# Hybrid decoder step: paged value loads in another token order, and four edits to the order of the attention work

## Chip, cores and metric

One Trainium2 chip, one NeuronCore. The metric is the device time of one execution of the whole program in microseconds (us), lower is better.

## The reference

Two layers; each is a half-step SwiGLU feed-forward (FFN), a mixing stage and a second half-step FFN. There are two groups of rows: a prompt (1 sequence of 256 tokens) and a sample group (8 sequences of 8 new tokens, each with 1024 cached tokens). Cut to the mixing stage:

```python
z = rmsnorm(x, g_mix) @ w_in                   # 1024 -> 2944 columns: u | qa ka va | qr kr vr gr
y_pool, pool_new = pool_mixer(u, ...)          # 4 groups x 64
past_k = cache_k[l][page_table].reshape(8, 1024, 6, 64)    # 8 pages of 128 tokens per sequence
past_v = cache_v[l][page_table].reshape(8, 1024, 6, 64)
y_att = moba_seq(q, concat(past_k, ka), concat(past_v, va), pos)
    # blocks of 256 keys, each query takes its 3 best past blocks (by q . mean key) and its own,
    # s = q.k / 8 - slope_h * distance, softmax, p @ v
o_r, ret_new = retention(qr, kr / 8, vr, s0)   # chunkwise recurrent, per-head norm, silu gate
x = x + concat(y_pool, y_att, y_ret) @ w_out
```

All of it is float32. Softmax and p @ v add over the keys of a sequence, so the order in which the 128 tokens of a page stand is free as long as scores, distance penalty and values use the same one.

## The kernel before

**The work.** 1024x256-column chunks of weights are loaded by SP's queue (1 MB each, `w_raw`), split by ACT (`w_hi`, L702) and DVE (`w_lo`, L1024; four chunks of the mixing stage by POOL, L643) into two fp32r parts, and multiplied on PE in three passes (L1477 to L1479 in the FFNs, L1597 to L1599 as `mix(c)` for the chunks 0 to 11 of the mixing projection, L1929 to L1931 as the output projection). The moving side is 320 rows: 256 of the prompt, 64 of the sample group.

**The mixing stage** is an order written out by hand for each engine: between the chunks of `mix` stand the parts of the attentions whose inputs are ready. For the sample group's attention the 8 sequences go in 4 pairs p = 0 to 3. Per pair:
- SP and POOL load 16 pages of K, 192 KB each (L410; a page's 128 tokens go to 32 partitions as `"(t r) h d -> t r (h d)"`, four neighbouring tokens to a partition), DVE turns them (`turn_k`, L1143, two halves per sequence), and PE multiplies 48 times (`sample_scores(p)`: L1745 the cached keys, L1757 the new ones) into PSUM banks 2 and 3. There the four tokens of a partition come out as `r t`: token t*4+r is column 32*r+t of its page.
- DVE adds the penalty (`soft_in(p)`, L1215 to L1222; L1216 is the large addition, which at the same time writes the columns back from `r t` into `t r`, the tokens' own order), then finds blocks, maxima and biases (`soft_bias`), and ACT takes the exponentials (`exps(p, parts)`, L861, nine parts).
- PE transposes the probabilities (L1766, L1772) and multiplies them with the value pages (`smp_out(p)`, L1791). The 8 pages of sequence u are loaded by SP (u = 0, 3, 4, 6; L472 and L473) or POOL (u = 1, 2, 5, 7; L656 and L657), 128 tokens to 128 partitions, 1536 bytes each. `smp_out(p)` waits on the arrival counts of all pages of u = 2p and 2p + 1.

The prompt's attention has 6 heads: scores (`scores(i)`, two heads), the maxima of them on DVE (`smax(h)`, L1174 to L1178, which counts `s_max`), exponentials on ACT, transposes on PE (`transpose_p`, L1667). The sample scores of pairs 1, 2 and 3 wait on `s_max`, and `scores(0)` on `sm_in`, which `soft_in` counts.

**SP's queue** in the mixing stage: K pages of pair 1, weight chunks 3 to 6, ..., K pages of pair 3 after `sample_scores(2)` has counted `sc_done`, V pages of u = 0, V pages of u = 3 and 4 after the scores of pair 3, two chunks of `w_out` after `smp_out(0)`, V pages of u = 6, stores of the retention states (L489, L494), two more chunks of `w_out`, then the weights of the second FFN. DMAs of a queue are issued in that order and are not waited for.

**ACT's queue** carries five small loads at the start (L750 to L754): gains, as 16, 16, 16, 8 and 4 rows of 512 bytes.

The V loads differ from the K loads in the pattern only:

```python
A["cache_k"][L, page[j]].rearrange("(t r) h d -> t r (h d)", r=4)   # L411, K: 32 x 4 x 384
A["cache_v"][L, page[j]].rearrange("t h d -> t (h d)")              # L473, L657, V: 128 x 384
```

Of the kernel before, what the change touches and what calls it, by code (L numbers as in the profile page):

```python
# [16 lines left out]
ALU = mybir.AluOpType  # L17
# [13 lines left out]
H = 6  # L31
# [82 lines left out]
def build(nc, A, C, O):  # L114
    ctx = ExitStack()

    def sb(name, shape, dt=F32):
        return ctx.enter_context(nc.sbuf_tensor(name, shape, dt))
# [4 lines left out]
    with ctx:  # L123
# [12 lines left out]
        cst = {n: sb(n, list(C[n].shape)) for n in C}  # L136
# [66 lines left out]
        sp = [sp_a, sp_b, sp_d, sp_a]  # L203
# [52 lines left out]
        s_done, s_max, s_exp, p_norm = sem("s_done"), sem("s_max"), sem("s_exp"), sem("p_norm")  # L256
# [13 lines left out]
        v_landed = {n: sem("v_landed_" + n) for n in "QCWXABDE"}  # L270
        V_HOME = "XQWABCED"
# [85 lines left out]
        def _(sp_e):  # L357
# [43 lines left out]
            for L in range(DEPTH):  # L401
# [65 lines left out]
                def load_v(u, n=PAGES, halves=range(2)):  # L467

                    for half in halves:
                        page = page_numbers(mybir.EngineType.SP, u * PAGES + 4 * half, min(4, n - 4 * half))  # L470
                        for j in range(min(4, n - 4 * half)):
                            sp_e.dma_start(v_page(u, 4 * half + j, slice(0, HDIM)),  # L472
                                           A["cache_v"][L, page[j]].rearrange("t h d -> t (h d)")).then_inc(v_landed[V_HOME[u]], 16)  # L473

                for half in range(2):
                    wait_apart(sp_e, split_done, L * C_ALL + (C_MIX + half + 13))
# [44 lines left out]
        def _(pool):  # L521
# [47 lines left out]
            for L in range(DEPTH):  # L569
# [39 lines left out]
                for n, w in enumerate(WINDOWS):  # L609
# [8 lines left out]
                    o, t = HD * (n % 2), n // 2  # L618
# [34 lines left out]
                def load_v(u, half, first=0, n=4):  # L653
                    page = page_numbers(mybir.EngineType.Pool, u * PAGES + 4 * half + first, n)
                    for j in range(n):
                        pool.dma_start(v_page(u, 4 * half + first + j, slice(0, HDIM)),  # L656
                                       A["cache_v"][L, page[j]].rearrange("t h d -> t (h d)")).then_inc(v_landed[V_HOME[u]], 16)  # L657

                for c in range(8, 12):
                    mix_lo(c)  # L660
# [36 lines left out]
        def _(act):  # L697
# [88 lines left out]
            for L in range(DEPTH):  # L786
# [34 lines left out]
                def vr_tokens(t):  # L821
                    n = P if t < 2 else SMP
                    act.wait_ge(vr_tr, 3 * L + (t + 1))
                    act.activation(vr_tok[0:n, t, :], ps[0:n, VR_BANK[t], 0:HDIM], ACT.Copy).then_inc(vr_out, 1)
# [29 lines left out]
                def exps(p, parts=range(9)):  # L854
                    if 0 in parts:
                        act.wait_ge(sm_bias, L * 4 + p + 1)
                    for k in parts:
                        n, part = divmod(k, 3)
                        a, b = (256 * n + P * part, 256 * n + P * part + P) if part < 2 else (768 + 32 * n, 800 + 32 * n)
                        at_b = 32 * part + n  # L860
                        ins = act.activation(sp[p][:, a:b], sp[p][:, a:b], ACT.Exp, bias=bias_s[:, at_b:at_b + 1],  # L861
                                             accum_out=blk[:, at_b:at_b + 1])
                    if 8 in parts:
                        ins.then_inc(sm_exp, 1)
# [77 lines left out]
                probs_out(5)  # L942
                act.wait_ge(evac_done, L * G_ALL + (GROUPS0 + G_MIX + 12))
                act.activation(z[:, ZG:ZG + 3, :], z[:, ZG:ZG + 3, :], ACT.Silu).then_inc(g_silu, 1)
                exps(3, range(4))
                out_evac(0)
                act.wait_ge(stored_va, 16 * (L + 1))
                att_evac(2)
                exps(3, range(4, 9))
                for t in range(3):  # L950
                    vr_tokens(t)
                for t in range(2):
                    act.wait_ge(pool_mm, 2 * L + (t + 1))
                    act.activation(h_hi[:, t, :], ps[:, 6 + t, 0:TOK], ACT.Copy, scale=gains[:, bass.ds(L * 2 + (NORMS * KT + t), 1)]).then_inc(pool_hi, 1)
# [65 lines left out]
        def _(dve):  # L1020
# [113 lines left out]
            for L in range(DEPTH):  # L1134
# [4 lines left out]
                def turn_k(p, bb, half):  # L1139

                    dve.wait_ge((k_landed[k_home(p, bb)] if p else k_first[bb])[half], k_count(L, p))
                    keys = kbuf[k_home(p, bb)][:, 4 * half:4 * half + 4, :].rearrange("p j c -> p (j c)")
                    dve.transpose(keys, keys).then_inc(kt_ok, 1)  # L1143
# [12 lines left out]
                def evac_first(c):  # L1156
                    dve.wait_ge(tile_done, L * 11 + (c + 1))
                    to_z(2 * c, 2 if c == 1 else 0).then_inc(mix_half, 1)
# [6 lines left out]
                def mix_lo(c):  # L1165
                    lo_split(half0 + (C_MIX + c) // 2, c % 2)
# [44 lines left out]
                def soft_in(p):  # L1211

                    dve.wait_ge(own_done, L * 4 + p + 1)
                    raw = ps[:, 2:4, :].rearrange("p b n -> p (b n)")
                    dve.tensor_reduce(past_blocks(0), raw[:, 0:768].rearrange("p (n k x) -> p n k x", n=3, k=2), AX, ALU.add)  # L1215
                    dve.tensor_tensor(sp[p][:, 0:768].rearrange("p (k t r) -> p k r t", k=6, r=4),  # L1216
                                      raw[:, 0:768].rearrange("p (k r t) -> p k r t", k=6, r=4),
                                      cst["alibi_s"][:].rearrange("p (k r t) -> p k r t", k=6, r=4), ALU.add)
                    dve.tensor_tensor(sp[p][:, 768:864], raw[:, 768:864], cst["alibi_own"][:, p, :], ALU.add).then_inc(sm_in, 1)
                    dve.drain()  # L1220
                    dve.tensor_reduce(past_blocks(2), sp[p][:, 0:768].rearrange("p (n k x) -> p n k x", n=3, k=2), AX, ALU.max)
                    dve.tensor_reduce(blk[:, 128:131], sp[p][:, 768:864].rearrange("p (n x) -> p n x", n=3), AX, ALU.max)  # L1222
                    dve.drain()
# [80 lines left out]
                soft_bias(0)  # L1304
                evac_last(4)
                turn_k(1, 1, 0)
                mix_lo(6)
                turn_k(1, 1, 1)
                smax(0)
                dve.drain()  # L1310
                smax(1)
# [32 lines left out]
                                                cst["q_decay"][o:o + HD, f, :].rearrange("p (b t) -> p b t", b=NB), ALU.mult)  # L1344
                ins.then_inc(q_dec_ok, 1)
                dve.wait_ge(stored_u, 32 * (L + 1))
                soft_in(2)
                evac_first(9)
                soft_bias(2)
                evac_last(9)  # L1350
                turn_k(3, 0, 0)
# [112 lines left out]
        def _(pe):  # L1464
# [102 lines left out]
            for L in range(DEPTH):  # L1567
# [7 lines left out]
                def mix(c, tiles=None):  # L1575

                    if not tiles or 0 in tiles:
                        chunk_split(half0 + (C_MIX + c) // 2, c % 2)
                    tiles = tiles or range(2 if c < 11 else 1)
                    steps = [(a, k) for a in tiles for k in range(KT)]  # L1580
                    if c == 0:
                        steps.sort(key=lambda step: step[1] // 2)
                    for a, k in steps:
                        if c in FETCH and a == tiles[-1] and a == 1 and k == 3:
                            pe.addr_align(BLOCK, FETCH[c], 0)
                        if k == 0:
                            if c < 2:
                                banks_free(L, G_MIX)
                            elif a == 0:
                                pe.wait_ge(mix_half, L * 11 + c)  # L1590
                            else:
                                pe.wait_ge(evac_done, L * G_ALL + (GROUPS0 + G_MIX + c))
                        if c == 0 and a == 0 and k % 2 == 0:
                            pe.wait_ge(gx_ready, (norm + 1) * 4 + (k // 2 + 1))
                        w = slice((k * (2 if c < 11 else 1) + a) * P, (k * (2 if c < 11 else 1) + a + 1) * P)
                        out = ps[:, a + (2 if c == 1 else 0), 0:TOK]
                        pe.matmul(out, w_hi[:, c % 2, w], h_hi[:, k, :], start=(k == 0), stop=False)  # L1597
                        pe.matmul(out, w_hi[:, c % 2, w], h_lo[:, k, :], start=False, stop=False)  # L1598
                        ins = pe.matmul(out, w_lo[:, c % 2, w], h_hi[:, k, :], start=False, stop=(k == KT - 1))  # L1599
                        if k == KT - 1:  # L1600
                            ins.then_inc(tile_done if a == 0 and c < 11 else chunk_used, 1)
# [230 lines left out]
                mixed(4)  # L1832
                u_tokens()
                tokens(ZKA, 0, 7).then_inc(ka_tr, 1)
                pe.wait_ge(sm_in, L * 4 + 1)
                scores(0)
                mix(5)
                pe.wait_ge(ka_out, 3 * L + 1)
                tokens(ZKA, 1, 7).then_inc(ka_tr, 1)
                pe.wait_ge(s_max, H * L + 2)  # L1840
                sample_scores(1)
                mix(6)
                mixed(6)
# [9 lines left out]
                pe.wait_ge(va_out, 3 * L + 2)  # L1853
                att_out(0)
                tokens(ZVA, 2, 6).then_inc(va_tr, 1)
                pe.wait_ge(s_max, H * L + 4)
                sample_scores(2)
                mix(9)
                pe.wait_ge(oa_out, 3 * L + 1)
                tokens(ZKA, 2, 7).then_inc(ka_tr, 1)  # L1860
                transpose_p(2)
# [9 lines left out]
                att_out(1)  # L1871
                transpose_p(4)
                transpose_p(5)
                pe.wait_ge(s_max, H * L + 6)
                sample_scores(3)
                mix(11)

# [150 lines left out]
```

## Time and profile before

| | |
|---|---|
| runs, us | 1321.41, 1322.69, 1322.31 (median 1322.31) |
| profiled execution, us | 1318.97 (span 1317.1, mean granted PE clock 0.995) |
| busy share of the span | PE 98%, DVE 60%, ACT 50%, POOL 18% |
| first FFN and mixing stage, layer 0 | 0 to 254.5 us, 254.5 to 404 us |
| second FFN of layer 0 and first of layer 1 | 404 to 899.7 us |
| mixing stage and second FFN, layer 1 | 899.7 to 1051 us, 1051 to 1317 us |

The profile is of one execution. Its span is the time from the first to the last instruction; 1.9 us of the execution lie outside it. A row of a timeline gives start, duration, engine, line, operation, output and inputs, and in brackets how long the engine was idle before it and what released it. "SPq" and "POOLq" rows are the issue of a DMA, not its transfer. In a view of windows, "DMA" is the mean busy share of the core's 16 DMA engines, GB/s what they moved; records that straddle a window's edge can bring it over 1. PEclk is the TensorE clock that was granted, as a share of full speed (2.4 GHz).

### The profile page before, as it was taken

Reading aid. Unit: us, or ns where it says so; the run is one execution under the profiler, and the core shown is the slowest. Engines: PE = TensorE matmul, PEld = TensorE weight load, DVE = VectorE, ACT = ScalarE, POOL = GpSimd, SP = SyncE. Lnnn points to the kernel's source line nnn. Section 1 sums busy time; section 2 is a strip of 40 time slices with the busy share of each in tenths; the row PEclk is TensorE's granted clock in tenths of the full one; section 3 lists DMA queues with packets and bytes.
Section 4 is the critical chain, followed back from the end, with each engine's and each line's share of the span. In section 5 each row is a group of like instructions: output and inputs, shape, how many; then the busy total and the mean of one; then the engine's idle time right before and its main releaser. Section 6 shows DMA issues by size and latency. Waiting matters only on the chain.

```text
span 1317.1 us, 25155 instructions
## 1 busy us (share of the span) xinstructions
PE 1291.6 (98%) x9881; PEld 1243.8 (94%) x9881; DVE 787.9 (60%) x885; ACT 660.3 (50%) x838; POOL 237.3 (18%) x389
## 2 busy tenths in 40 slices
PE   9999999998999999999999999999899999999998
PEld 7999999997869999999999999999797799999998
DVE  6555555677876655554465555566877675555433
ACT  6555543345464655543365554333446455555433
POOL 1021000358541000000110000013855220000010
PEclk9999999999999999999999999999899999999999
DMA  6676544668994444444456554447599834444441
GB/s 202 203 199 193 167 140 153 187 171 209 284 343 156 136 159 149 138 152 144 151 166 187 165 183 145 150 150 202 142 253 311 292 128 160 144 143 159 144 148 68
DMA packets 201671, 232.97 MB, mean 177 GB/s; under 512 B 15006, under 2 KB 192936, under 8 KB 201604
## 3 DMA queue, kind: packets, MB, share of 16 engines
q1 hardware_dynamic: 194172, 209.10, 51.1%
q0 software_dynamic: 7312, 22.95, 5.9%
q8 instruction: 42, 0.69, 0.2%
q14 instruction: 25, 0.20, 0.1%
q10 hardware_dynamic: 120, 0.03, 0.0%
HBM read 226.83 MB, written 5.32 MB: 176 GB/s over the span
## 4 chain that ended last, share of the span: by engine, by line
PE 85%; DVE 6%; DMA 2%; ACT 2%; DVEq 2%; issue 1%; SPq 1%; ACTq 0%
PE ps L1477 24%; PE ps L1478 24%; PE ps L1479 24%; DMA kbuf<-in_cache_k 2%; PE ps L1597 2%; PE ps L1599 2%; PE ps L1598 2%; DVE w_lo L1024 1%; PE ps L1745 1%; SPq L410 1%; DVE kbuf L1143 1%; PE ps L1929 1%; ACT w_hi L702 1%; DVEq L1220 1%; PE ps L1931 1%
## 5 line engine op out<-in xcount | busy, mean ns | idle before, releaser
L702 ACT ACTIVATE w_hi<-w_raw 128x2048 fp32r<-128x2048 f32 x167 | 319.9, 1915 | 514.3 <-PE ps L1479 415.2
L1024 DVE TENSOR_TENSOR w_lo<-w_raw,w_hi 128x2048 fp32r<-128x2048 f32 x159 | 365.9, 2301 | 196.5 <-ACT w_hi L702 192.0
L1477 PE MATMUL ps<-h_hi,w_hi 128*128 128x320 f32 x768 | 237.9, 310 | 0.8 <-DVE h_lo L1112 0.7
L1479 PE MATMUL ps<-h_hi,w_lo 128*128 128x320 f32 x768 | 237.3, 309 | 0.0
L1478 PE MATMUL ps<-h_lo,w_hi 128*128 128x320 f32 x768 | 237.3, 309 | 0.0
L1477 PE MATMUL ps<-g_hi,w_hi 128*128 128x320 f32 x704 | 217.9, 309 | 0.0
L1479 PE MATMUL ps<-g_hi,w_lo 128*128 128x320 f32 x704 | 217.4, 309 | 0.0
L1478 PE MATMUL ps<-g_lo,w_hi 128*128 128x320 f32 x704 | 217.4, 309 | 0.0
L1478 PE MATMUL ps<-act_lo,w_hi 128*128 128x320 f32 x704 | 217.2, 309 | 0.0
L1477 PE MATMUL ps<-act_hi,w_hi 128*128 128x320 f32 x704 | 217.2, 309 | 0.0
L1479 PE MATMUL ps<-act_hi,w_lo 128*128 128x320 f32 x704 | 217.2, 309 | 0.0
L1477 PEld LDWEIGHTS ps<-h_hi,w_hi 128*128 128x128 f32 x768 | 144.2, 188 | 2.1 <-issue 1.5
L1478 PEld LDWEIGHTS ps<-h_lo,w_hi 128*128 128x128 f32 x768 | 144.2, 188 | 0.1
L1479 PEld LDWEIGHTS ps<-h_hi,w_lo 128*128 128x128 f32 x768 | 144.2, 188 | 0.0
L1477 PEld LDWEIGHTS ps<-g_hi,w_hi 128*128 128x128 f32 x704 | 132.4, 188 | 0.2
L1478 PEld LDWEIGHTS ps<-g_lo,w_hi 128*128 128x128 f32 x704 | 132.3, 188 | 0.2
L1479 PEld LDWEIGHTS ps<-g_hi,w_lo 128*128 128x128 f32 x704 | 132.4, 188 | 0.0
L1478 PEld LDWEIGHTS ps<-act_lo,w_hi 128*128 128x128 f32 x704 | 132.0, 187 | 0.0
L1477 PEld LDWEIGHTS ps<-act_hi,w_hi 128*128 128x128 f32 x704 | 132.0, 187 | 0.0
L1479 PEld LDWEIGHTS ps<-act_hi,w_lo 128*128 128x128 f32 x704 | 132.0, 187 | 0.0
L1597 PE MATMUL ps<-h_hi,w_hi 128*128 128x320 f32 x368 | 116.4, 316 | 0.2 <-DVE z L1154 0.2
L1599 PE MATMUL ps<-h_hi,w_lo 128*128 128x320 f32 x368 | 113.7, 309 | 0.0
(309 smaller groups left out, 1764.0 us busy)
## 6 DMA issues: line engine op xcount, KB each, us to landing
w_raw<-in_ffn_w_in SPq DMA_DIRECT2D x87, 1024.0 KB, 5.1
w_raw<-in_ffn_w_out SPq DMA_DIRECT2D x32, 896.0 KB, 4.6
w_raw<-in_w_in SPq DMA_DIRECT2D x22, 1024.0 KB, 5.4
kbuf<-in_cache_k SPq DMA_DIRECT2D x96, 192.0 KB, 5.1
w_raw<-in_ffn_w_out SPq DMA_DIRECT2D x16, 1024.0 KB, 4.9
w_raw<-in_w_out SPq DMA_DIRECT2D x8, 1024.0 KB, 7.0
kbuf<-in_cache_k POOLq DMA_DIRECT2D x32, 192.0 KB, 3.7
kbuf<-in_cache_v SPq DMA_DIRECT2D x32, 192.0 KB, 5.1
```

Source lines behind the costliest of these rows:

```text
L410: sp_e.dma_start(kbuf[home][32 * j:32 * j + 32, 4 * half:4 * half + 4, :], A["cache_k"][L, page[j]].rearrange("(t r) h d -> t r (h d)", r= ...
L702: act.activation(w_hi[:, slot, :], w_raw[:, slot, :], ACT.Copy).then_inc(hi_done, 1)
L1024: dve.tensor_tensor(w_lo[:, slot, :], w_raw[:, slot, :], w_hi[:, slot, :].bitcast(F32), ALU.subtract).then_inc(split_done, 1)
L1143: dve.transpose(keys, keys).then_inc(kt_ok, 1)
L1220: dve.drain()
L1477: pe.matmul(out, w_hi[:, slot, w], hi[:, k, :], start=(k == 0), stop=False)
L1478: pe.matmul(out, w_hi[:, slot, w], lo[:, k, :], start=False, stop=False)
L1479: ins = pe.matmul(out, w_lo[:, slot, w], hi[:, k, :], start=False, stop=(k == k_all - 1))
L1597: pe.matmul(out, w_hi[:, c % 2, w], h_hi[:, k, :], start=(k == 0), stop=False)
L1598: pe.matmul(out, w_hi[:, c % 2, w], h_lo[:, k, :], start=False, stop=False)
L1599: ins = pe.matmul(out, w_lo[:, c % 2, w], h_hi[:, k, :], start=False, stop=(k == KT - 1))
L1745: ins = pe.matmul(ps[32 * g:32 * g + 32, 2 + n // 2, 256 * (n % 2):256 * (n % 2) + 256], q_sc[p][:, at_q:at_q + 32], kbuf[k_home(p, g // 2 ...
```

## The change

1. Both V loads read a page as `"(t r) h d -> r t (h d)"`: partition 32*r+t gets token 4*t+r.
2. `soft_in` adds the penalty without reordering: 128x768 on all three sides, contiguous.
3. Four waits on PE are gone (`sm_in` before `scores(0)`, `s_max` before the sample scores of pairs 1, 2 and 3), and the scores of pair 2 move to between the two halves of `mix(9)`. (Pairs count from 0: p = 2 is the third.)
4. On DVE, `turn_k(1, 1, 1)` goes ahead of `mix_lo(6)`, and `evac_first(9)` ahead of `soft_in(2)`.
5. On ACT, the exponentials of pair 3 come as 2 parts, then (behind `att_evac(2)` and the three `vr_tokens`) 7 parts, where there were 4, 5 and then `vr_tokens`.

```diff
 def load_v(u, ...):      # once on SP (L473), once on POOL (L657)
-    A["cache_v"][L, page[j]].rearrange("t h d -> t (h d)")
+    A["cache_v"][L, page[j]].rearrange("(t r) h d -> r t (h d)", r=4)

 def soft_in(p):          # DVE
-    dve.tensor_tensor(sp[p][:, 0:768].rearrange("p (k t r) -> p k r t", k=6, r=4),
-                      raw[:, 0:768].rearrange("p (k r t) -> p k r t", k=6, r=4),
-                      cst["alibi_s"][:].rearrange("p (k r t) -> p k r t", k=6, r=4), ALU.add)
+    dve.tensor_tensor(sp[p][:, 0:768], raw[:, 0:768], cst["alibi_s"][:], ALU.add)

 # ACT
-    exps(3, range(4))
+    exps(3, range(2))
     out_evac(0)
     act.wait_ge(stored_va, 16 * (L + 1))
     att_evac(2)
-    exps(3, range(4, 9))
     for t in range(3):
         vr_tokens(t)
+    exps(3, range(2, 9))

 # DVE
+    turn_k(1, 1, 1)
     mix_lo(6)
-    turn_k(1, 1, 1)
...
+    evac_first(9)
     soft_in(2)
-    evac_first(9)

 # PE
-    pe.wait_ge(sm_in, L * 4 + 1)
     scores(0)
...
-    pe.wait_ge(s_max, H * L + 2)
     sample_scores(1)
...
-    pe.wait_ge(s_max, H * L + 4)
+    mix(9, (0,))
     sample_scores(2)
-    mix(9)
+    mix(9, (1,))
...
-    pe.wait_ge(s_max, H * L + 6)
     sample_scores(3)
```

Order of the instructions on SP's queue at the first V pages (the layer's loop body; the shape is that of the DMA's pattern), before and then of the change:

```order
160 L472 DMA w_raw<-in_cache_v 128x384
161 L472 ISA
162 L472 DMA w_raw<-in_cache_v 128x384
163 L472 ISA
```

```order
160 L472 DMA w_raw<-in_cache_v 128x1x384
161 L472 ISA
162 L472 DMA w_raw<-in_cache_v 128x1x384
163 L472 ISA
```

Nothing moved on SP; only the pattern is another. In the program as built, the DRAM side of a page was 128 rows of 384 elements; it is now 4 (384 elements apart) by 32 (1536 apart) by 384, the outermost dimension being the 4. The SBUF side keeps its 128 partitions outermost.

Order on DVE ahead of the scores of pair 1 (`kbuf_59` is the K buffer of the pair's second sequence), before and then of the change:

```order
93 L1143 STREAM_TRANSPOSE kbuf_59<-kbuf_59 128x1536
94 L1024 TENSOR_TENSOR w_lo<-w_raw,w_hi 128x2048
95 L1143 STREAM_TRANSPOSE kbuf_59<-kbuf_59 128x1536
96 L1174 SCALAR_TENSOR_TENSOR s_p<-dist_p,ps 128x384
```

```order
93 L1143 STREAM_TRANSPOSE kbuf_59<-kbuf_59 128x1536 x2
94 L1024 TENSOR_TENSOR w_lo<-w_raw,w_hi 128x2048
95 L1174 SCALAR_TENSOR_TENSOR s_p<-dist_p,ps 128x384
```

The second turn now stands ahead of the split of chunk 6, so the scores of pair 1 have their keys one L1024 earlier.

Order on PE at the scores of pair 2, behind the 64-row transposes of the sample group's values (L1638), before and then of the change (whose lines stand two lower from there on):

```order
977 L1638 MATMUL ps<-ident,z 64x128 x3
978 L1745 MATMUL ps<-kbuf_60,tmp 32x256 [waits sm_in,kt_ok,qp_ok,s_max]
...
991 L1757 MATMUL ps<-k_own,q_bd 32x32 [waits qb_ok]
992 L1757 MATMUL ps<-k_own,q_bd 32x32 x11
993 L1597 MATMUL ps<-h_hi,w_hi 128x320 [waits mix_half,split_done]
```

```order
976 L1636 MATMUL ps<-ident,z 64x128 x3
977 L1595 MATMUL ps<-h_hi,w_hi 128x320 [waits mix_half,split_done]
...
1001 L1743 MATMUL ps<-kbuf_60,tmp 32x256 [waits kt_ok,sm_in,qp_ok]
...
1015 L1755 MATMUL ps<-k_own,q_bd 32x32 x11
1016 L1595 MATMUL ps<-h_hi,w_hi 128x320 [waits evac_done]
```

24 matmuls (half of `mix(9)`) moved ahead of the scores, and the wait on `s_max` is gone.

## Rows read from the trace of the kernel before

**Rows 1.** Page, part 1: busy us, share of the span, instructions.

```profile
PE 1291.6 (98%) x9881; PEld 1243.8 (94%) x9881; DVE 787.9 (60%) x885; ACT 660.3 (50%) x838; POOL 237.3 (18%) x389
```

**Rows 2.** Windows by stage: window, length, busy (x instructions) per engine, PEclk, DMA share, GB/s.

```profile
254.50:404.00 149.50, 140.98 (x1523) 121.08 (x1522) 113.91 (x232) 75.39 (x206) 81.13 (x143) 0.99 0.85 246
404.00:671.00 267.00, 267.00 (x1818) 266.68 (x1818) 148.06 (x109) 135.07 (x111) 16.15 (x14) 1.00 0.45 148
899.70:1051.00 151.30, 142.43 (x1521) 121.11 (x1520) 114.46 (x231) 75.15 (x206) 78.94 (x143) 0.98 0.84 243
```

**Rows 3.** Waits of PE: released by, us in total, times, longest.

```profile
PE ps L1745 <- DVE st L1178: 7.2, 2, 3.9
PE ps L1745 <- DVE kbuf L1143: 2.8, 2, 1.7
```

**Rows 4.** Timeline of PE: scores of pair 1 in both layers, pair 2.

```profile
300.03 4.21 PE L1745 MATMUL ps<-kbuf,q_sc_b 128*32 128x256 f32 x48 [3.35 <-DVE st L1178]
...
331.02 2.80 PE L1745 MATMUL ps<-kbuf,tmp 128*32 128x256 f32 x48 [1.68 <-DVE kbuf L1143]
...
946.05 5.35 PE L1745 MATMUL ps<-kbuf,q_sc_b 128*32 128x256 f32 x48 [3.89 <-DVE st L1178]
```

**Rows 5.** Windows around the scores: pair 1 in both layers, pair 2.

```profile
300.00:304.20 4.20, 4.17 (x68) 2.13 (x72) 2.38 (x5) 4.19 (x10) 3.84 (x7) 0.65 0.12 38
...
946.00:951.40 5.40, 5.35 (x64) 2.61 (x68) 3.51 (x6) 4.55 (x10) 3.51 (x6) 0.50 0.08 28
331.00:333.80 2.80, 2.78 (x70) 2.10 (x72) 2.31 (x11) 1.02 (x1) 0.00 (x0) 1.00 1.04 348
```

**Rows 6.** Timeline of SP: issue of K pages of pair 3, V pages, output weights.

```profile
334.63 9.41 SPq L410 DMA_DIRECT2D kbuf<-in_cache_k  x16
...
345.98 5.24 SPq L472 DMA_DIRECT2D w_raw<-in_cache_v  x8
357.90 10.71 SPq L472 DMA_DIRECT2D kbuf<-in_cache_v  x16
368.80 1.97 SPq L365 DMA_DIRECT2D w_raw<-in_w_out  x2
376.57 4.85 SPq L472 DMA_DIRECT2D v_e<-in_cache_v  x8
...
384.35 9.63 SPq L494 DMA_DIRECT2D out_ret_sample<-s  x6
394.02 7.57 SPq L365 DMA_DIRECT2D w_raw<-in_w_out  x2
```

**Rows 7.** Page, part 3: a DMA queue, its packets, MB, share.

```profile
q10 hardware_dynamic: 120, 0.03, 0.0%
```

**Rows 8.** Issues of DMAs on ACT's queue: xcount, KB each.

```profile
g_rows<-in_norm_ffn ACTq DMA_DIRECT2D x2, 8.0 KB
g_rows<-in_norm_mix ACTq DMA_DIRECT2D x1, 8.0 KB
g_rows<-in_norm_final ACTq DMA_DIRECT2D x1, 4.0 KB
g_rows<-in_pool_scale ACTq DMA_DIRECT2D x1, 2.0 KB
```

**Rows 9.** Windows of 5 us: K pages landing (first), V pages landing (the other two).

```profile
320.00:325.00 5.00, 5.00 (x37) 4.99 (x36) 2.21 (x5) 4.31 (x10) 2.18 (x2) 1.00 1.05 217
350.00:355.00 5.00, 4.31 (x41) 3.25 (x43) 4.77 (x10) 4.32 (x19) 3.29 (x6) 1.00 1.07 382
365.00:370.00 5.00, 3.39 (x34) 2.83 (x30) 3.03 (x13) 4.26 (x22) 0.00 (x0) 1.00 1.01 345
```

**Rows 10.** Timeline of PE: first use of the V pages, first output chunk of the second half.

```profile
361.13 0.35 PE L1791 MATMUL ps<-w_raw,pt_s 128*24 128x192 f32 x2
...
397.72 0.35 PE L1791 MATMUL ps<-v_e,tmp 128*24 128x192 f32 x2
...
401.23 0.41 PE L1929 MATMUL ps<-h_hi,w_hi 128*128 128x320 f32 x1 [0.25 <-DVE w_lo L1024]
```

**Rows 11.** Groups of instructions: the two splits of a chunk.

```profile
L702 ACT ACTIVATE w_hi<-w_raw 128x2048 fp32r<-128x2048 f32 x167 | 319.9, 1915 | 514.3 <-PE ps L1479 415.2
L1024 DVE TENSOR_TENSOR w_lo<-w_raw,w_hi 128x2048 fp32r<-128x2048 f32 x159 | 365.9, 2301 | 196.5 <-ACT w_hi L702 192.0
```

**Rows 12.** Groups by form on DVE: the strided addition, contiguous passes of its width.

```profile
L1215 DVE TENSOR_REDUCE blk<-ps 128x6 f32<-128x768 f32 x8 | 7.6, 948 | 4.2 <-PE ps L1757 4.2
L1216 DVE TENSOR_TENSOR sp_a<-ps,alibi_s 128x768 f32<-128x768 f32 x4 | 6.2, 1544 | 0.0
L1388 DVE TENSOR_TENSOR h_lo<-z,h_hi 128x768 fp32r<-128x768 f32 x2 | 1.9, 948 | 0.0
```

**Rows 13.** Timelines of POOL and DVE: split of chunk 8, turn of pair 3's last keys.

```profile
314.72 5.09 POOL L643 TENSOR_TENSOR w_lo<-w_raw,w_hi 128x512 fp32r<-128x512 f32 x4
...
351.80 1.78 DVE L1143 STREAM_TRANSPOSE kbuf<-kbuf 128x1536 f32<-128x1536 f32 x1
```

**Rows 14.** L472 by source: DMA to landing us min/median/max.

```profile
DMA to landing us min/median/max: 3.5/5.5/10.6
```

More of the change, by code:

```diff
@@ L472, in load_v @@
                             sp_e.dma_start(v_page(u, 4 * half + j, slice(0, HDIM)),
-                                           A["cache_v"][L, page[j]].rearrange("t h d -> t (h d)")).then_inc(v_landed[V_HOME[u]], 16)
+                                           A["cache_v"][L, page[j]].rearrange("(t r) h d -> r t (h d)", r=4)).then_inc(v_landed[V_HOME[u]], 16)
                 for half in range(2):
@@ L656, in load_v @@
                         pool.dma_start(v_page(u, 4 * half + first + j, slice(0, HDIM)),
-                                       A["cache_v"][L, page[j]].rearrange("t h d -> t (h d)")).then_inc(v_landed[V_HOME[u]], 16)
+                                       A["cache_v"][L, page[j]].rearrange("(t r) h d -> r t (h d)", r=4)).then_inc(v_landed[V_HOME[u]], 16)
                 for c in range(8, 12):
```

## The prediction

> **What bounds the kernel now.** I read the busy shares first: PE is busy 98% of the span [rows 1]. The windows by stage say where the other 2% are: the FFNs leave nothing, the two mixing stages leave 149.5 - 141.0 = 8.5 and 151.3 - 142.4 = 8.9 us [rows 2]. What an attention edit can win is in those 17 us, and in matmuls at a reduced clock. The waits of PE name the holes: 7.2 us ahead of pair 1's scores, released by a prompt maximum on DVE, 2.8 us ahead of later scores, released by the turn of the keys [rows 3]. The timeline adds the clock: behind its hole the block of 48 matmuls takes 4.21 us in layer 0 and 5.35 us in layer 1, where pair 2's same block takes 2.80 us [rows 4]. The granted clock of those stretches is 0.65 and 0.50 of full speed (1.2 in place of 2.4 GHz for most or all of it) against 1.00 [rows 5]. Last I read the DMAs, because the change touches 128 of them, and a mixing stage keeps the 16 DMA engines busy 85% of its time [rows 2]. That is where this forecast is decided.
>
> **The V loads: how many DMA engines carry one.** The pattern keeps the bytes, the 1536-byte rows and the place of every DMA in its queue, but makes a dimension of 4 the outermost one in DRAM. The nearest evidence is ACT's queue: it shows 120 packets [rows 7] for its five loads [rows 8], which have 16, 16, 16, 8 and 4 rows outermost, 60 in all. If each DMA engine that takes part closes its share with one completion packet, five DMAs on 16 engines would make 60 + 80 = 140 packets; 60 + (16 + 16 + 16 + 8 + 4) = 120 is what stands there. So a DMA of 4 outermost rows runs on 4 engines. The packet records of the two `pool_sample` stores (8 outermost each) say more: the second's packets stand behind the first's on the same 8 engines, so short DMAs of a queue don't take turns over all 16. I conclude that each V page of the change goes over 4 engines, and that all of SP's pages go over the same 4.
>
> The Trainium skill, "DMA: Bandwidth & Descriptors", in the section "Why a DMA increments its semaphore by 16 and not by 1", has the same as a rule: the number of engines is the largest one up to 16 that divides the slowest dimension of both sides, here of 4 and 128, and a hardware queue uses the lowest-numbered ones. By that rule the change loses three quarters of the bandwidth on these pages; by the skill's 16-engine case it would lose nothing. The trace agrees as far as it goes (120 packets, not 140); no run here shows a page with 4 outermost.
>
> **The price of a page.** 196.6 KB over 4 engines. While V pages land now, the 16 engines move 345 to 382 GB/s, 21.6 to 23.9 GB/s each; while K pages land (32 partitions, all engines full) 217 GB/s, 13.6 each [rows 9]. So a page takes at the least 196.6 / (4 x 23.9) = 2.06 us, at the most 196.6 / (4 x 13.6) = 3.62 us. I take 2.5 us: the nearest row is V's own, with the same 1536-byte rows, but I allow for the four engines writing four groups of 32 partitions in step.
>
> **Sum of one layer.** Every page of SP goes into the line of those four engines, behind the K pages of pair 3, whose issue ends at 344 us; V starts at about 347.5 [rows 6].
> - SP's 32 pages: 32 x 2.5 = 80 us (66 to 116).
> - POOL's 32 pages, with a queue of their own, take a share. Spread evenly they cost each of the 16 engines 196.6 / 16 / 22.8 = 0.54 us a page, 17.3 us.
> - Two chunks of `w_out`, ahead of the pages of u = 6: 2 x 1.05 MB / 16 / 22.8 = 5.8 us on each engine.
> - Sum 347.5 + 80 + 17.3 + 5.8 = 450.6, and 1.5 us from the last byte to PE: pair 3's `smp_out`, which waits for u = 6, starts at 452.1. It starts at 397.72 now [rows 10]. That is 54.4 us late (39 with a page at 2.06 and the shares at 23.9, 90 with 3.62).
> - Behind the pages of u = 6 come the retention stores (0.79 MB, 2.1 us) and the second half of `w_out` (2.9 us for its first chunk), then ACT's and DVE's split of it, 1.92 + 2.30 us [rows 11]. The first matmuls on it come 9.2 us after that `smp_out` starts, now 3.5 us [rows 10]: 5.7 us more.
> - PE has waited long by then, several times (the first `smp_out`, at 361.1 now, needs u = 0's eight pages, which end at 347.5 + 8 x 3.04 = 371.8 at the earliest). Each restart costs what rows 4 show, 1.4 to 2.5 us; I take 1.5 a layer, since the waits run into each other.
>
> 61.6 us a layer, 123 in two. The FFN behind has no slack to give back: PE is busy in all of its 267 us, and its DMA share of 0.45 [rows 2] only says that the weights catch up soon.
>
> **The other edits**, worth something only if the V loads stay harmless:
> - L1216 becomes contiguous: 1544 ns to the 948 ns of passes of its width [rows 12], 8 x 0.6 = 4.8 us of DVE. PE waits for DVE elsewhere, so some of it shows.
> - The four waits and `turn_k(1, 1, 1)`: the scores of pair 1 start 3.5 us earlier and run at full clock, `mix(6)` thus 4.6 and 5.7 us earlier. But DVE has to do the same splits and evacuations; by its own chain the chunks that follow come only about 1.2 us earlier, and chunk 8 is split by POOL from 314.7 to 319.8 [rows 13], whatever PE does. So 1.1 to 1.2 us a layer survive.
> - The scores of pair 2, half a chunk (3.6 us) later: PE's 1.7 us wait for the keys [rows 4] is covered. Yet `sc_done` of pair 2 frees pair 3's K buffers, and their turn already starts just as the last page lands (issued to 344.0, turned at 351.80 [rows 6, 13]). By my reckoning those scores end 0.85 us later in layer 0, and 0.9 to 2.2 earlier in layer 1.
> - ACT: `vr_tokens` before most exponentials of pair 3 takes 0.7 us of waiting away from the pooled output and makes it wait for the same engine later. Nothing.
>
> These give -2.5 to +1 us in all, taken as -1. With V late they lie under its wait.
>
> Profiled execution 1318.97 + 123.2 - 1 = 1441. It lies 3.3 below the median of the runs, so the forecast for the median is **1444 us**.
>
> **Rivals.**
> - *A: the pages spread after all* (the compiler or the queue cuts a page into more pieces, or successive pages take other engines). For it: landing pages overlap, and four at a time on 4 engines each would fill 16; no row has a run of 4-engine DMAs. Against it: the 120 packets and the stacked stores. Then the remaining edits rule: 1322.3 - 1 = 1321 us, range 1319.5 to 1323.5, within 0.2% (2.6 us), which is about what a measurement of this kernel can tell from no change. Chance 7%.
> - *B: faster.* The pages spread, and the time won ahead of pair 1 is kept, because DVE, 0.6 us lighter per pair and with its turn moved up, hands its splits on earlier. Place: PE at L1745. Price: 7.2 + 2.8 us of waits [rows 3] and (4.21 - 2.80) + (5.35 - 2.80) = 4.0 us of clock [rows 4], 14 us: 1308. It decides from the point where `mix(8)` starts more than 1.3 us a layer earlier. Against it: rows 13. Chance 5%.
> - *C: the four engines are slow or fast.* Same mechanism, other price. At 2.06 us a page: 2 x (39 + 5.7 + 1) = 91, 1413. At 3.62: 2 x (90 + 6.5 + 2) = 197, 1518. Within my forecast's chance.
> - *D: only latency.* Pages take other engines in turn, but each lands later by 2 us or so: pair 0's `smp_out`, whose eight pages were issued from 346.0, has a reserve of 361.1 - 351.2 = 9.9 us over the last issue [rows 6, 10] against landings of 3.5 to 10.6 us now [rows 14]. Up to 2 us a layer: 1322 to 1326. It is in the chances of same and slower.
>
> **Chances.** V pages bound to four engines: 86% (1400 to 1515, most likely 1444). D 2%, A 7%, B 5%. Slower by over 0.2%: 0.86 + half of D and a little of A = 0.88; within 0.2%: 0.07; faster 0.05. The range leaves out A, B and D (14%) and so has to hold nearly all of the main case: its bounds are C's two prices, opened to 1390 below, since four engines may run faster when the other twelve idle.
>
> **What would show it.** In the windows of the changed kernel at 350 to 450 us: DMA share near 0.25 and 60 to 95 GB/s, where now 1.01 to 1.07 stand [rows 9]. PE idle ahead of L1789 (`smp_out`, two lines up) in each layer, released by DMAs of `cache_v` that SP issued. Landing of SP's V pages tens of us in place of 3.5 to 10.6. L1216 at 0.95 us. Pair 1's block of L1743 at 2.8 us in both layers. Wrong would be: DMA share still near 1 at 350 to 390 us with pages landing within 11 us (then A, B or D), or the wait sitting on POOL's pages.

## The result and the profile after

The changed kernel takes 1442.58 us (median of 4 runs, 1441.21 to 1444.40) against 1321.86 us for the kernel before beside it: ratio 1.092, 95% interval 1.090 to 1.094. The profiled execution has a span of 1441.6 us, 124.5 more than before.

The page of the changed kernel, its busy shares, DMA queues and part of the chain that ended last:

```profile
PE 1311.1 (91%) x9881; PEld 1256.9 (87%) x9881; DVE 786.7 (55%) x885; ACT 661.5 (46%) x838; POOL 246.0 (17%) x389
...
q1 hardware_dynamic: 193404, 209.09, 47.3%
q0 software_dynamic: 15504, 23.04, 7.3%
...
PE 76%; SPq 15%; DVE 2%; POOL 2%; issue 2%; DMA 2%; POOLq 1%; DVEq 1%; ACT 0%; ACTq 0%
```

PE's share falls from 98% [rows 1] to 91%, and 15% of the chain is now SP's queue: issuing DMAs, which was 1% before. The queue of SP (q1) carries 768 packets fewer than before (194172 then), with the same bytes. 768 is 64 x 12: each of SP's 64 value pages closes with 4 completion packets in place of 16, as the five small loads of [rows 7, 8] suggested. POOL's queue (q0) went from 7312 packets to 15504, 128 more for each of its 64 pages.

Waits of PE in the changed kernel (released by, us in total, times, longest):

```profile
PE ps L1789 <- DMA w_raw<-in_cache_v: 42.9, 2, 22.6
PE ps L1789 <- DMA kbuf<-in_cache_v: 40.3, 2, 20.8
PE ps L1789 <- DMA v_e<-in_cache_v: 20.7, 2, 10.9
PE ps L1764 <- DVE o_past L1353: 6.2, 2, 3.2
PE ps L1595 <- DVE z L1154: 5.4, 7, 1.8
PE ps L1708 <- DVE h_lo L1378: 4.2, 2, 2.1
```

The account closes with these. Three waits for SP's values (u = 0, 4 and 6) make 103.9 us. PE is busy 19.5 us longer with the same 9881 matmuls, all of it a lower granted clock (0.954 against 0.995). The waits for `st` and `kbuf` of [rows 3], 10.0 us, are gone, and the last three lines, 15.8 us, are all but new (0.6 us before). Small waits for `o_tok`, `s_p` and `vr_tok`, 5.5 us before, don't appear any more. That makes 103.9 + 19.5 - 10.0 - 5.5 + 15.8 = 123.7, of 124.5; what is left are waits of under 1 us.

SP's queue in layer 0, to be laid beside [rows 6]:

```profile
335.67 10.43 SPq L410 DMA_DIRECT2D kbuf<-in_cache_k  x16
...
348.06 19.22 SPq L472 DMA_DIRECT2D w_raw<-in_cache_v  x8
368.32 46.09 SPq L472 DMA_DIRECT2D kbuf<-in_cache_v  x16
414.61 16.41 SPq L365 DMA_DIRECT2D w_raw<-in_w_out  x2
431.84 15.62 SPq L472 DMA_DIRECT2D v_e<-in_cache_v  x8
```

The issue itself is held up now: 16 pages took 10.71 us to issue, and take 46.09. From 376 to 396 us SP issues a page every 2.0 us, which is also the pace at which pages land, with some four issued and not yet landed. So it seems that the queue takes a few pages, and then has a place only when one has drained. The issue comes to (19.22 + 46.09 + 15.62) / 32 = 2.53 us a page. That is not what a page costs by itself, since POOL's traffic is in it: from 350 to 375 us SP's queue moves 1.23 MB beside 3.06 MB of POOL's, some 4.0 us a page, and from 380 to 395 us, when POOL's queue moves nothing, 1.44 MB, 2.05 us a page.

Windows of the changed kernel (columns as in [rows 2]), where [rows 9] had a DMA share over 1 at 345 to 382 GB/s:

```profile
365.00:375.00 10.00, 0.00 (x0) 0.00 (x0) 1.50 (x9) 1.40 (x5) 1.41 (x3) 0.56 0.58 140
375.00:385.00 10.00, 2.03 (x28) 1.40 (x32) 0.00 (x0) 0.00 (x0) 0.00 (x0) 0.50 0.27 96
385.00:395.00 10.00, 9.07 (x106) 6.54 (x98) 2.80 (x9) 4.67 (x20) 2.43 (x5) 0.92 0.28 97
```

From 375 to 395 us POOL issues no page, SP's pages are issued as fast as the queue takes them, and the DMA share is 0.27: as much as four engines of 16, at 24 GB/s each. If pages that follow each other used other engines, the share would rise with the number in flight; it doesn't, so they use the same four. The trace's packet records name no engine, but they show how many packets run at once: from 380 to 395 us nearly always four or five of SP's value pages, in the kernel before (350 to 354 us) mostly 15 to 18. A 1536-byte packet takes 69 ns in the mean there, and took 67, so each of the four engines runs as fast as before.

PE's timeline (as in [rows 10]):

```profile
382.97 0.52 PE L1789 MATMUL ps<-w_raw,pt_s 128*24 128x192 f32 x2 [20.32 <-DMA w_raw<-in_cache_v]
...
435.66 0.52 PE L1789 MATMUL ps<-kbuf,pt_s 128*24 128x192 f32 x2 [19.55 <-DMA kbuf<-in_cache_v]
...
457.19 0.52 PE L1789 MATMUL ps<-v_e,tmp 128*24 128x192 f32 x2 [9.82 <-DMA v_e<-in_cache_v]
```

Each matmul behind such a wait takes 0.52 us where it took 0.35 at full clock [rows 10].

### The profile page after: what moved, and what is told of

Read it like the earlier page. It is cut to its first block, busy times and chain, and to the rows that moved or that the text cites. A ratio compares the mean times of both kernels' runs of the same rounds, so it can differ in the third digit from the quotient of the medians.

```text
span 1441.6 us, 25149 instructions
## 1 busy us (share of the span) xinstructions
PE 1311.1 (91%) x9881; PEld 1256.9 (87%) x9881; DVE 786.7 (55%) x885; ACT 661.5 (46%) x838; POOL 246.0 (17%) x389
## 3 DMA queue, kind: packets, MB, share of 16 engines
q0 software_dynamic: 15504, 23.04, 7.3%
## 4 chain that ended last, share of the span: by engine, by line
PE 76%; SPq 15%; DVE 2%; POOL 2%; issue 2%; DMA 2%; POOLq 1%; DVEq 1%; ACT 0%; ACTq 0%
PE ps L1475 22%; PE ps L1477 22%; PE ps L1476 22%; SPq L472 10%; SPq L365 2%; PE ps L1595 2%; PE ps L1596 2%; PE ps L1597 2%; DMA v_e<-in_cache_v 2%; SPq L410 1%; SPq L342 1%; PE ps L1789 1%; PE ps L1548 1%; PE ps L1924 1%; PE ps L1926 0%
## 5 line engine op out<-in xcount | busy, mean ns | idle before, releaser
L1024 DVE TENSOR_TENSOR w_lo<-w_raw,w_hi 128x2048 fp32r<-128x2048 f32 x159 | 365.7, 2300 | 240.2 <-ACT w_hi L702 235.7
L1477 PE MATMUL ps<-h_hi,w_lo 128*128 128x320 f32 x768 | 237.3, 309 | 0.0
L1476 PE MATMUL ps<-h_lo,w_hi 128*128 128x320 f32 x768 | 237.3, 309 | 0.0
L1596 PE MATMUL ps<-h_lo,w_hi 128*128 128x320 f32 x368 | 114.6, 312 | 0.0
```

The costliest lines, as they stand in the source:

```text
L1024: dve.tensor_tensor(w_lo[:, slot, :], w_raw[:, slot, :], w_hi[:, slot, :].bitcast(F32), ALU.subtract).then_inc(split_done, 1)
L1476: pe.matmul(out, w_hi[:, slot, w], lo[:, k, :], start=False, stop=False)
L1477: ins = pe.matmul(out, w_lo[:, slot, w], hi[:, k, :], start=False, stop=(k == k_all - 1))
```

## The experiments

Twelve kernels were run, each against the kernel before on the same chip. The kernel before gave 1319.36 us (e1 to e4), 1319.55 (e5 to e8) and 1319.79 (e9 to e12).

### e1 to e4: which pages, and how many engines

**e1**, parts 1 and 2 of the change on the kernel before:

```diff
-    A["cache_v"][L, page[j]].rearrange("t h d -> t (h d)")                  # SP and POOL
+    A["cache_v"][L, page[j]].rearrange("(t r) h d -> r t (h d)", r=4)
-    dve.tensor_tensor(sp[p] as (k t r), raw as (k r t), alibi_s as (k r t), ALU.add)
+    dve.tensor_tensor(sp[p][:, 0:768], raw[:, 0:768], cst["alibi_s"][:], ALU.add)
```

> The kernel before with parts 1 and 2 of the change alone (value pattern on SP and POOL, contiguous penalty addition); no wait or order is changed. Theory T (SP's value pages run on four DMA engines and their line sets the end of the mixing stage): as slow as the whole change, 1435 to 1446 us. Rival S (the new order of the scores pushes key and value loads into each other and makes a good part of the loss): under 1400 us.

Measured: 1443.86 us, ratio 1.095 (1.093 to 1.097). The value pattern, with the addition that belongs to it, makes the whole loss; rival S falls. Under the late values the reordering of parts 3 to 5 shows neither way.

**e2** and **e3**, the changed kernel with the new pattern left on one queue only:

```diff
 # e2, POOL (L657) back; e3, SP (L473) back
-    A["cache_v"][L, page[j]].rearrange("(t r) h d -> r t (h d)", r=4)
+    A["cache_v"][L, page[j]].rearrange("t h d -> t (h d)")
```

> The changed kernel with the old pattern on POOL's 64 value pages, the new one on SP's 64; so the tokens of u = 1, 2, 5, 7 stand in another order than their probabilities. Theory T: nearly all of the loss stays, 1415 to 1443 us. Rival P (POOL's software queue, whose packets went from 7312 to 15504, is what costs): near the kernel before, 1320 to 1335 us. SP issue of 16 pages at L472 still 40 us or more by T, some 11 us by P.

> The changed kernel with the old pattern on SP's 64 value pages, the new one on POOL's 64; so the tokens of u = 0, 3, 4, 6 stand in another order than their probabilities. Theory T: 1318 to 1335 us, since POOL's pages share no line of four engines. Rival P: 1400 to 1443 us.

Measured: e2 1416.43 us, ratio 1.073 (1.072 to 1.075); e3 1364.30 us, ratio 1.033 (1.031 to 1.035). e2 stands as theory T had it: SP's pages carry most of the loss. e3 misses its range by 29 us: POOL's pages cost too, and not through the line of four. A window of e2, a window of e3, and e3's waits of PE:

```profile
375.00:380.00 5.00, 0.75 (x12) 0.56 (x16) 0.00 (x0) 0.00 (x0) 0.00 (x0) 0.50 0.27 97
```

```profile
365.00:370.00 5.00, 0.00 (x0) 0.00 (x0) 1.70 (x10) 1.66 (x5) 1.68 (x3) 0.67 1.03 175
```

```profile
PE ps L1789 <- DMA v_q<-in_cache_v: 13.0, 2, 7.7
PE ps L1789 <- DMA v_c<-in_cache_v: 8.4, 2, 4.9
PE ps L1789 <- DMA v_d<-in_cache_v: 7.4, 2, 3.9
```

In e2 the share is that of four engines again. In e3 all 16 are busy and move 175 GB/s, half of the 345 of [rows 9] with the same share: POOL's pages are spread over all engines in the mean, but while they land everything is slow, SP's own pages too (landing 4.3 / 15.7 / 20.2 us min, median and max, against 3.5 / 5.5 / 10.6 [rows 14]). The Trainium skill ("DMA: Bandwidth & Descriptors", section "Why a DMA increments its semaphore by 16 and not by 1") says that a software queue picks k consecutive engines from a round-robin cursor, where a hardware queue takes the lowest k. The two windows agree with that: 0.27 against 1.03. Why the busy engines move only half is open; no run here took SBUF's side apart.

**e4**, r = 8 in both patterns:

```diff
-    A["cache_v"][L, page[j]].rearrange("(t r) h d -> r t (h d)", r=4)
+    A["cache_v"][L, page[j]].rearrange("(t r) h d -> r t (h d)", r=8)
```

> The changed kernel with r = 8 in place of 4 in both value patterns (8 outermost in DRAM); the tokens of a page stand in another order than their probabilities. Theory T: the price of a page halves, 1.2 to 1.4 us in place of 2.4 to 2.9, so the last values come 0 to 12 us late in a layer: 1320 to 1345 us. Rival G (it is the strided rows of the DRAM side that cost, whatever their outer number): as slow as the change, 1435 to 1445 us.

Measured: 1378.82 us, ratio 1.045 (1.043 to 1.046). A window of e4:

```profile
370.00:375.00 5.00, 0.00 (x0) 0.00 (x0) 0.00 (x0) 0.00 (x0) 0.00 (x0) 0.50 0.53 190
```

Share 0.53 and 190 GB/s: eight engines at 24 GB/s. SP's queue has 512 packets fewer than before (193660), 8 a page. The number of engines follows the outer dimension, and rival G (as slow as the change) falls. My range was too low by 34 us. At 190 GB/s a page by itself takes 1.03 us, half of what it takes with r = 4. SP needed (7.31 + 24.61 + 23.66) / 32 = 1.74 us a page all the same, since POOL's pages land as well, and then both are slow, as in e3.

### e5 to e8: sixteen engines, and the rest of the change

**e5**, the same with r=16. **e7**, the changed kernel with the old value pattern. **e6**, parts 3 to 5 of the change on the kernel before. **e8**, the tokens put in order on the side of the keys:

```diff
 # e8: values as before the change, and
-    A["cache_k"][L, page[j]].rearrange("(t r) h d -> t r (h d)", r=4)
+    A["cache_k"][L, page[j]].rearrange("(r t) h d -> t r (h d)", r=4)
-key_at = PAGE * (...) + 4 * tok_t[None] + tok_r[None]
+key_at = PAGE * (...) + tok_t[None] + 32 * tok_r[None]
```

> The changed kernel with r = 16 in both value patterns (16 outermost in DRAM, strided rows all the same); the tokens of a page stand in another order than their probabilities. Theory T: no loss from SP's pages, 1317 to 1325 us. Rival G (strided rows cost whatever the outer number): 1435 to 1445 us. A loss of 3 to 15 us would be POOL's queue, whose descriptors are of the new kind here too.

> The kernel before with parts 3 to 5 of the change alone (PE's waits, the place of the pair-2 scores, DVE's and ACT's order); values and penalty addition as before. My sum: -2 to +2 us against the kernel before (1320 to 1324). Rival B (the waits that go are won in full): 1306 to 1312 us.

> The changed kernel with the old value pattern; so the tokens stand in another order than their probabilities. My sum: -2.5 to +1 us against the kernel before (1319 to 1323). Rival B: 1304 to 1311 us. The difference to e6 is the contiguous penalty addition alone: 0 to 3 us less.

> The same layout of the scores got from the other side: K pages read as (r t) h d -> t r (h d), so that column 32*r+t is token 32*r+t, the table of distances to match, and values in their own order with the old pattern (all else as in the change). Outermost 32 in DRAM, so 16 engines; the K packets become 1536 bytes in place of 6144. Theory T: as e7 within 3 us if the 32 partitions limit K pages anyway (217 to 257 GB/s now). Rival K (small packets slow K pages): 5 to 20 us slower than e7, with PE or DVE waiting for K pages ahead of the scores.

| | us | ratio (95% interval) |
|---|---|---|
| e5, 16 engines, strided rows | 1336.05 | 1.0125 (1.0108 to 1.0142) |
| e6, order alone | 1331.67 | 1.0088 (1.0067 to 1.0108) |
| e7, all but the values | 1326.11 | 1.0052 (1.0030 to 1.0074) |
| e8, keys in order | 1325.92 | 1.0048 (1.0032 to 1.0064) |

With 4, 8 and 16 outermost rows the kernel takes 1442.6, 1378.8 and 1336.1 us: theory T's order, with nine tenths of the loss over e7 gone at 16. But e5 is 11 us above the range that I gave it. 6.6 of its 16.5 us are e7's; in the other 10 the pages land later on both queues (SP's after 8.1 us in the median, in e7 5.4; POOL's 7.3 and 5.2), though POOL's queue has its 7312 packets of before. They belong to the strided rows themselves or to how POOL's queue carries them; no run separates the two. e8 has the layout that the change wanted, with each probability beside its own value, at e7's time: it keeps 32 rows outermost in DRAM, and 1536-byte packets for K pages cost nothing that shows.

What I had wrong is e6 and e7: parts 3 to 5 lose 12 us, and 6.6 with the contiguous addition, where I had -2 to +2 and -2.5 to +1. (That the addition wins the difference is likely, not certain: the runs of e6 go from 1327.6 to 1336.7 us, those of e7 from 1322.2 to 1333.2.) PE's timelines of e6 in layer 0 show two new waits:

```profile
348.64 1.54 PE L1766 MATMUL ps<-ident,sp_a 128*128 128x128 f32 x6 [3.73 <-DVE o_past L1355]
...
376.20 0.45 PE L1710 MATMUL ps<-vr_tok,kr_tok 128*64 128x64 f32 x8 [2.12 <-DVE h_lo L1380]
```

The wait ahead of pair 1's scores (3.35 us, at 300) has become one of 3.73 us at 345, and behind it the clock falls just the same (L1766 takes 1.54 us, 0.81 before). Windows of e7 and of the kernel before for the second one:

```profile
376.00:380.00 4.00, 4.00 (x37) 3.34 (x38) 2.58 (x9) 1.92 (x3) 1.89 (x5) 0.50 1.09 358
380.00:384.00 4.00, 4.00 (x31) 2.76 (x31) 0.85 (x4) 1.26 (x6) 0.85 (x2) 0.50 1.04 368
```

```profile
376.00:380.00 4.00, 4.00 (x61) 2.87 (x56) 2.54 (x9) 2.70 (x11) 2.56 (x5) 1.00 1.09 362
380.00:384.00 4.00, 3.86 (x43) 2.50 (x40) 2.52 (x5) 1.71 (x4) 0.84 (x2) 1.00 1.04 366
```

In these 8 us e7 gets 68 matmuls done at a clock of 0.50 (1.2 GHz), the kernel before 104 at 1.00. What each engine did before it fell: PE had been idle 2.13 us at 372.5 to 374.7, where before the same gap came as 1.47 and 0.69 us with matmuls between.

### e9 to e12: the parts of the order

```diff
 # e9: the kernel before with part 5 alone
-    exps(3, range(4)); out_evac(0); ...; att_evac(2); exps(3, range(4, 9)); vr_tokens(0..2)
+    exps(3, range(2)); out_evac(0); ...; att_evac(2); vr_tokens(0..2); exps(3, range(2, 9))
 # e10: the kernel before with parts 3 and 4 alone
 # e11: the kernel before with e8's K pattern and table, and part 2
 # e12: e11 with parts 3 and 4
```

> The kernel before with part 5 of the change alone (ACT: vr_tokens ahead of seven parts of the exponentials of pair 3). e6 and e7 show a wait of 2.1 us at the second retention step (released by h_lo on DVE, which follows ACT) and behind it some 9 us at half the PE clock in each layer. Theory A (this part alone brings that): 1325 to 1331 us, with the wait in the profile. Rival O (the scores of pair 2 behind half of mix(9) bring it, by making everything later): within 2 us of the kernel before.

> The kernel before with parts 3 and 4 of the change alone (PE's waits and the place of the scores of pair 2; DVE's turn and evacuation). Theory A: 1316 to 1321 us. Rival O: 1326 to 1332 us.

> The kernel before with keys in token order by the K load, the table of distances to match and the contiguous penalty addition; all orders as before. 4.8 us less DVE work, of which e6 against e7 gave back 5.5 us: 1314 to 1319 us. If the 1536-byte K packets cost what the addition wins: 1319 to 1323 us.

> e8 with ACT's order as before: keys in token order, contiguous addition, parts 3 and 4. Theory A: 7 to 12 us under e8's 1325.9, 1311 to 1319 us, and as fast as or faster than both kernels of the case. Rival O: 1322 to 1327 us.

| | us | ratio (95% interval) |
|---|---|---|
| e9, ACT's order | 1323.62 | 1.0021 (1.0003 to 1.0040) |
| e10, PE's and DVE's order | 1326.48 | 1.0044 (1.0029 to 1.0060) |
| e11, layout alone | 1320.96 | 1.0003 (0.9989 to 1.0018) |
| e12, layout, PE's and DVE's order | 1321.33 | 1.0010 (0.9998 to 1.0023) |

Neither theory holds alone. e9 is below theory A's range and outside rival O's; e10 is in O's range; e12 lies between the two. ACT's order costs 0.2% on the kernel before, just clear of nothing, and 4.6 us on e12 (e8 against e12). PE's and DVE's order costs 0.4% on the kernel before; the two alone, 3.8 and 6.7 us, come near e6's 12.1. With the contiguous addition PE's and DVE's order costs next to nothing (e12 against e11, 0.4 us): in that order the addition wins 5.2 us (e10 against e12), and in the old one nothing (e11, for which I had 1314 to 1319). e9 brings the 2.1 us wait, as theory A said, but in its profiled execution the clock stayed at 1.00 in the window behind it (PE's timeline, then the window):

```profile
374.38 0.45 PE L1710 MATMUL ps<-vr_tok,kr_tok 128*64 128x64 f32 x8 [2.12 <-DVE h_lo L1380]
```

```profile
376.00:386.00 10.00, 9.65 (x118) 6.97 (x115) 6.82 (x14) 5.27 (x17) 3.67 (x8) 1.00 1.06 364
```

So the same wait is followed by a clock of 0.50 in layer 0 of e7, and by 1.00 in layer 1 of the same execution (1028 to 1038 us), in both layers of e9 and in layer 0 of e8. It would fit a spread of these kernels' runs (e9 1318.1 to 1330.0, e7 1322.2 to 1333.2), but the kernel before spreads nearly as far (1316.5 to 1326.8), and that the spread comes from there was not shown.

e10 has the loss without that wait. Its waits of PE that are new or longer:

```profile
PE ps L1597 <- DVE z L1154: 7.9, 7, 3.7
PE ps L1766 <- DVE o_past L1355: 7.9, 2, 4.2
PE ps L1667 <- DVE sp_b L1219: 2.0, 2, 1.0
```

They make 17.8 us, where the kernel before had 0.6 on these lines and 10.0 on the waits that are gone: 7.2 us more, and e10 is 6.7 slower. `z` is the evacuation of a chunk of `mix`: PE comes to the next chunk sooner, and stands there until DVE has emptied its bank. In e12, with 0.6 us less for DVE per pair, `z` is down to 6.0 and `o_past` to 6.9.

For the longer one, `o_past`, the rows of DVE from the scores of pair 2 on (e10):

```profile
334.76 0.96 DVE L1215 TENSOR_REDUCE blk<-ps 128x6 f32<-128x768 f32 x1 [1.51 <-PE ps L1757]
335.63 1.54 DVE L1216 TENSOR_TENSOR sp_d<-ps,alibi_s 128x768 f32<-128x768 f32 x1
...
344.09 0.45 DVE L1154 TENSOR_TENSOR z<-ps,rstd 128x320 f32<-128x320 f32 x1
344.47 3.42 DVE L1143 STREAM_TRANSPOSE kbuf<-kbuf 128x1536 f32<-128x1536 f32 x2
347.81 0.58 DVE L1355 COPY o_past<-ps 128x192 f32<-128x192 f32 x2
```

DVE needs 13.6 us from the scores of pair 2 to `o_past`: penalty, blocks, biases, an evacuation, two turns. Before, PE had all of `mix(9)` and more to do in that time. With half of `mix(9)` ahead of the scores it has half a chunk less, and waits 3.73 us in layer 0, 4.18 in layer 1. The move took away a wait of 1.68 us [rows 4] and made one of 3.73. None of the versions beats the kernel before; e11 is level with it.

## Why the prediction was right, point by point

- **The V loads run on four engines, the same ones.** Right, and now shown: 768 completion packets fewer, share 0.27 at 96 to 97 GB/s, and 8 engines for 8 outermost rows (e4). Rivals A, B and D needed the pages spread; they fell with it.
- **The price of a page**, 2.5 us: too high. By itself a page takes 2.05 us (380 to 395 us), C's lower price, and 32 of them 66 us, not 80. The four groups of 32 partitions, for which I had added something, cost nothing that shows. SP's 2.53 us of issue a page agree with 2.5 by chance: POOL's traffic is in them, which the sum counts once more in a term of its own.
- **POOL's share**, 17.3 us a layer as 32 pages spread evenly: too low. From the first issue to the last packet the line took 348.1 to 456.5 us, 108.4. Less 65.6 for SP's pages and 5.8 for `w_out` that leaves 37.0 for POOL's pages, with latency and short gaps. In e2, with POOL's old pattern, it leaves 26.0 (347.4 to 444.8). So even the plain pages weigh more than I gave them, and the new pattern adds 11. Its cost for the kernel is 38 us alone (e3 against e7) and 26 on top of SP's (1416.4 to 1442.6 us), since SP's line is the longer one. The first wait says the same: it ended at 382.97 us, where I had 371.8 at the earliest.
- **The line's end.** Forecast 452.1 us, measured 457.19. The mechanism was right; that the sum came so close is in part luck, because the term of SP's pages, 14.4 us too high, and that of POOL's, 19.7 too low, cancel but for 5.3.
- **Behind it**, 5.7 us a layer for the second half of `w_out`: wrong. The output matmuls on it start at 462.60, 5.4 us after that `smp_out` starts (3.5 before), so it cost 1.9. These 3.8 us too many nearly cancel the 5.1 too few at the line's end.
- **The clock**, 1.5 us a layer: as a sum over PE it is 19.5 us in all. Most of it lies ahead of the next late page, which PE would have had to wait for anyway; behind the last one of layer 0 the clock is at half for 4.6 us more, which costs up to 2.3.
- **The other edits**, -1 us: this step failed, hidden under the late values. e7 shows +6.6 (0.3 to 0.7%). I had let 1.1 to 1.2 us a layer survive of the waits that go; in e10 the 10.0 us of them come back as waits for the evacuations and for `o_past`, and more. I had reckoned the turn of pair 3's keys behind the moved scores, but not `o_past`, which stands behind it in DVE's order and for which PE waits; and I had called ACT's order nothing, where PE's steps wait for `h_lo` 2.1 us in one piece. The size of L1216 was right (948 ns).
- **What would show it**: landing was to be tens of us. The profile gives no landing for SP's value pages here. PE goes on 15.7, 21.2 and 9.7 us after SP has issued the last page of u = 0, 4 and 6, so the pages land later than before (3.5 to 10.6), and a good part of the waiting goes into the issue. POOL's pages landed after 2.6 / 8.1 / 16.7 us (min, median, max), before 3.0 / 5.2 / 8.2. The share, the waits at L1789, L1216 and pair 1's block at full clock came as said.

## What to carry to other kernels

Before a load's access pattern is changed, look at the outermost dimension on both sides: the bytes and SP's packet sizes stayed the same here, and the dimension of 4 made 16 DMA engines into 4 for SP's pages and cost 7.3% (e2, the other edits' 0.5% among them), with POOL's pages 9.2%. The number of completion packets on the page (768 fewer) gives it away, and so does a DMA share stuck at 0.25 or 0.5. If two tensors must agree in an order, move it on the side whose outermost dimension stays large, as e8 does with the keys. When a sum comes out, its terms still have to be measured one by one: the issue time of a page agreed with the forecast and held another queue's traffic. And a wait on an in-order engine that is removed by moving work ahead of it has to be followed to the next wait on that engine: there is now less work between.

## What I had not expected of the hardware

- SP's issue stalls when its pages are slow: 46.09 us for 16 issues, 10.71 before, at some four pages under way.
- POOL's pages with 4 outermost rows keep all 16 DMA engines busy (1.03) at half the rate (175 GB/s, 345 before), and make 128 more packets a page; with 8 outermost rows 48 more (q0: 10384), with 16 none (q0: 7312).
- A wait of 2.1 us in one piece on PE was followed by about 10 us at 1.2 GHz in layer 0 of e7 and by none in its layer 1, in the same program order.
